# A loop over experts that takes two rounds at a time and gathers the tokens of both with one set of 256-column products

## The reference, cut to what matters

```python
def _moe(x, router, w_gate, w_up, w_down):
    xt = x.reshape(B * S, D)
    logits = (xt @ router).astype(jnp.float32)
    vals, ids = lax.top_k(logits, TOP_K)
    w = jax.nn.softmax(vals, axis=-1)
    gate = jnp.sum(jax.nn.one_hot(ids, N_EXPERTS, dtype=jnp.float32) * w[..., None], axis=1)
    out = jnp.zeros_like(xt)
    for e in range(N_EXPERTS):
        out = out + gate[:, e:e + 1].astype(xt.dtype) * _swiglu(xt, w_gate[e], w_up[e], w_down[e])
    return out.reshape(B, S, D)
```

## Time and profile before

| | |
|---|---|
| median of 3 runs | 2768.25 us (2766.36 to 2773.51) |
| the profiled execution | 2761.59 us, its span 2759.8 us |
| mean granted clock of TensorE | 0.988 of full speed |
| busy share of the span | TensorE 96%, VectorE 69%, ScalarE 55%, GpSimd 1% |
| moved from HBM | 578.8 MB, 210 GB/s over the span |
| expert rounds | 8, from 1751.83 to 2738.95 us of the span |

### The profile page before, as it was taken

One profiled execution on the slowest core, in us unless ns is written; L12 is line 12 of the kernel. 1 busy time (PEld: TensorE's weight loads), 2 busy tenths in 40 slices (PEclk: granted clock), 3 DMA queues, 4 the chain that ended last, 5 costly groups with the idle time before them and its releaser, 6 DMA issues.

```text
span 2759.8 us, 39481 instructions
## 1 busy us (share of the span) xinstructions
PE 2656.6 (96%) x14426; PEld 2179.9 (79%) x14426; DVE 1899.7 (69%) x2512; ACT 1515.8 (55%) x2207; POOL 18.1 (1%) x20
## 2 busy tenths in 40 slices
PE   7998999999998999989999999999999999999998
PEld 3754778888655999969999867888888888888887
DVE  2677555543258676575554656789898988989896
ACT  4223443222255544355444355678787877878785
POOL 0000000000000000000000100000000000000000
PEclk9999999999999999999999999999999999999999
DMA  6657122222220345314554222599899989889994
GB/s 259 238 198 310 62 92 92 103 96 92 92 77 31 138 170 183 137 62 153 184 184 153 107 77 107 210 347 379 338 373 354 365 349 370 350 338 375 346 370 168
DMA packets 80692, 581.53 MB, mean 211 GB/s; under 512 B 8896, under 2 KB 10176, under 8 KB 10176
## 3 DMA queue, kind: packets, MB, share of 16 engines
q1 hardware_dynamic: 80576, 579.90, 55.6%
HBM read 578.82 MB, written 1.05 MB: 210 GB/s over the span
## 4 chain that ended last, share of the span: by engine, by line
PE 87%; DVE 7%; ACT 3%; DMA 2%; issue 1%; POOL 0%; SPq 0%; ACTq 0%; DVEq 0%
PE ps L289 7%; PE ps L290 7%; PE ps L291 7%; PE ps L2483 7%; PE ps L2485 7%; PE ps L2484 7%; PE ps L2510 4%; PE ps L2512 4%; PE ps L2511 4%; PE ps L1118 3%; PE ps L1120 3%; PE ps L1119 3%; DMA ring<-in_stream_dram 2%; DVE parts L264 2%; PE ps L352 1%; PE ps L407 1%
## 5 line engine op out<-in xcount | busy, mean ns | idle before, releaser
L264 DVE TENSOR_TENSOR parts<-ring,parts 128x1024 fp32r<-128x1024 f32 x294 | 357.6, 1224 | 405.7 <-ACT parts L255 393.4
L255 ACT ACTIVATE parts<-ring 128x1024 fp32r<-128x1024 f32 x294 | 307.8, 1054 | 455.7 <-PE ps L291 195.7
L289 PE MATMUL ps<-parts 128*128 128x256 f32 (+1 forms) x1472 | 475.3, 323 | 7.9 <-DVE arena L1190 4.7
L290 PE MATMUL ps<-parts 128*128 128x256 f32 (+1 forms) x1472 | 470.7, 320 | 0.0
L291 PE MATMUL ps<-parts 128*128 128x256 f32 (+1 forms) x1472 | 470.3, 319 | 0.0
L2708 DVE TENSOR_TENSOR parts<-ring,parts 128x1024 fp32r<-128x1024 f32 x280 | 332.3, 1222 | 12.0 <-ACT parts L2551 0.4
L2551 ACT ACTIVATE parts<-ring 128x1024 fp32r<-128x1024 f32 x280 | 291.9, 1061 | 54.2 <-PE ps L2485 47.3
L289 PEld LDWEIGHTS ps<-parts 128*128 128x128 f32 x1472 | 281.3, 191 | 37.0 <-DVE arena L1190 8.1
L2483 PE MATMUL ps<-parts 128*128 128x512 f32 x752 | 296.8, 395 | 1.8 <-DVE parts L2708 1.8
L291 PEld LDWEIGHTS ps<-parts 128*128 128x128 f32 x1472 | 281.4, 191 | 19.8
L290 PEld LDWEIGHTS ps<-parts 128*128 128x128 f32 x1472 | 281.4, 191 | 19.6 <-issue 0.2
(11 more groups left out here) (400 smaller groups left out, 4692.3 us busy)
## 6 DMA issues: line engine op xcount, KB each, us to landing
ring<-in_stream_dram SPq DMA_DIRECT2D x380, 1024.0 KB, 5.8
h<-in_stream_dram SPq DMA_DIRECT2D x112, 1024.0 KB, 7.1
arena<-in_stream_dram SPq DMA_DIRECT2D x56, 1024.0 KB, 7.0
x<-in_x_dram SPq DMA_DIRECT2D x1, 2048.0 KB, 7.7
tab<-in_table_dram SPq DMA_DIRECT2D x1, 1724.5 KB, 11.7
out_dram<-x SPq DMA_DIRECT2D x4, 256.0 KB, 2.5
tab<-in_table_dram SPq DMA_DIRECT2D x1, 184.5 KB, 2.8
arena<-in_table_dram SPq DMA_DIRECT2D x1, 144.0 KB, 13.8
```

The costliest lines, as they stand in the source:

```text
L255: nc.scalar.activation(self.w_lead[:, self.buffer(g)], units(ring[:, n % NS, :])[:, g % UPS], ACT.Copy)\
L264: nc.vector.tensor_tensor(self.w_rest[:, self.buffer(g)], units(ring[:, n % NS, :])[:, g % UPS], self.w_lead[:, self.buffer(g)].bitcast(F3 ...
L289: nc.tensor.matmul(dst, wl[:, k, :], xl, start=(k == 0), stop=False)
L290: nc.tensor.matmul(dst, wl[:, k, :], xr, start=False, stop=False)
```

## The change

The loop now runs over pairs of rounds, and its body holds two rounds ("halves" 0 and 1) one behind the other. `Round(pair, half)` turns counts per round into semaphore values. The number of pairs is computed on VectorE beside the number of rounds, and an odd number of rounds is filled up with an empty one. `S_` has 256 columns, for the ranks of two rounds, and `select` makes all four blocks of it, in the second half alone. The gather is cut in two, `gather_lead` and `gather_rest`, 16 products of 256 columns each; both use banks 0 to 3, so `gather_rest` waits until ScalarE has copied the lead sums. In the second half the lead gather stands where the gather stood, at f = 14, and the rest gather stands at f = 18 (`LATE`); in the first half there is no gather. ScalarE and VectorE make four copies each (still 128 x 512) in the second half, VectorE's behind the cut of f = 23 (it was f = 19). There are two sets of `x_lead` and `x_rest`, the rests in a part of `x` that is free by then. Ahead of the loop, `gather_lead` comes before the six dummy products and `gather_rest` behind them. The places of `hidden_turn(NG - 1)`, `hidden_out(NG - 1)` and `hidden_rest(NG - 1)`, at f = 14, are the same in both halves.

```diff
@@ gather @@
-        def gather(eng):
-            for bank, tok in ((2, tok_lead), (0, tok_rest)):
-                for k in range(KD):
-                    for t in range(TT):
-                        mm = nc.tensor.matmul(ps[:, bank + k // 4, (k % 4) * P:(k % 4 + 1) * P], tok[:, t, k, :],
-                                              S_[:, t, :], start=(t == 0), stop=(t == TT - 1))
-                mm.then_inc(S("gathered"), 1)
+        def gather_lead(eng):
+            for k in range(KD):
+                for t in range(TT):
+                    mm = nc.tensor.matmul(ps[:, k // 2, (k % 2) * PS:(k % 2 + 1) * PS], tok_lead[:, t, k, :],
+                                          S_[:, t, :], start=(t == 0), stop=(t == TT - 1))
+            mm.then_inc(S("gathered"), 1)
+        def gather_rest(eng, pair):
+            for k in range(KD):
+                if k % 4 == 0:
+                    eng.wait_ge(S("x_lead"), pair * 4 + (2 * (k // 4) + 2))
+                for t in range(TT):
+                    mm = nc.tensor.matmul(ps[:, k // 2, (k % 2) * PS:(k % 2 + 1) * PS], tok_rest[:, t, k, :],
+                                          S_[:, t, :], start=(t == 0), stop=(t == TT - 1))
+            mm.then_inc(S("gathered"), 1)
@@ tensor, ahead of the loop @@
-            gather(eng)
+            gather_lead(eng)
...
+            gather_rest(eng, 0)
+            n = pair_count(eng)
@@ tensor, down cuts @@
                 for f in range(F2):
                     if f == F2 // 2:
                         hidden_turn(NG - 1)
-                        eng.wait_ge(S("sel"), r + 2)
-                        gather(eng)
+                        if at.half:
+                            eng.wait_ge(S("sel"), at.pair + 2)
+                            gather_lead(eng)
+                    if f == LATE and at.half:
+                        gather_rest(eng, at.pair + 1)
...
+            with eng.Fori(0, n) as pair:
+                for half in range(2):
+                    round_products(Round(pair, half))
@@ scalar @@
-                for m in range(2):
-                    tokens_lead(m, r + 1)
+                if at.half:
+                    tokens_lead(at.pair + 1)
@@ select, vector @@
+            for e in range(2):
+                for t in range(TT):
+                    ins = nc.vector.tensor_scalar(S_[:, t, e * P:(e + 1) * P], col("iota"), RK[:, t, of(e)], None,
+                                                  ALU.is_equal)
...
-                for i in range(NCU + F2 // 2, NCU + F2 // 2 + CUTS):
+                for i in range(NCU + F2 // 2, NCU + LATE + CUTS):
                     rest(i)
-                for m in range(2):
-                    tokens_rest(m, r + 1)
-                for i in range(NCU + F2 // 2 + CUTS, NC):
+                if at.half:
+                    tokens_rest(at.pair + 1)
+                for i in range(NCU + LATE + CUTS, NC):
                     rest(i)
```

More of the change, by code:

```diff
@@ L2325, in moe @@
         NCU, NC = 2 * NU, 2 * NSL
-        x_lead = parts[:, 0:UNIT].rearrange("p (k s) -> p k s", k=KD)
-        x_rest = parts[:, UNIT:2 * UNIT].rearrange("p (k s) -> p k s", k=KD)
+        x_leads, x_rests = ([parts[:, n * UNIT:(n + 1) * UNIT].rearrange("p (a b s) -> p a b s", a=4, b=2),
+                             x_r[:, 4 * n:4 * n + 4, T:NTOK].rearrange("p a (b s) -> p a b s", b=2)] for n in range(2))
         at = ARENA - 2 * F2 * P
@@ L2496, in tensor @@
                         mm.then_inc(S("sg_turn"), 1)
[L2498 removed]
+                eng.wait_ge(S("sum"), at(4, 6))
                 for f in range(F2):
@@ L2528, in scalar, with tokens_lead, outputs @@
             nc.scalar.activation(sm[:, 2:4], sm[:, 0:2], ACT.Exp).then_inc(S("exp"), 1)
[L2529 to L2537, removed]
+            def tokens_lead(pair):
+                eng.wait_ge(S("gathered"), pair * 2 + 1)
+                for n in range(2):
+                    for e in range(2):
+                        nc.scalar.activation(x_leads[e][:, 2 * n:2 * n + 2], gathered_half(n)[:, e], ACT.Copy)\
+                          .then_inc(S("x_lead"), 1)
+            def outputs(at):
+                eng.wait_ge(S("product"), at(NC, CUTS))
                 for n in range(2):
@@ L2699, in sums, with round_halves @@
                                             ALU.add).then_inc(signal, 1)
-            for m in range(2):
-                tokens_rest(m, 0)
-            n = round_count(eng)
-            with eng.Fori(0, n) as r:
+            tokens_rest(0)
+            n = pair_count(eng)
+            def round_halves(at):
                 def rest(i):
-                    eng.wait_ge(S("lead"), r * NC + (i + 1))
+                    eng.wait_ge(S("lead"), at(NC, i + 1))
                     nc.vector.tensor_tensor(w_rest[i % CUTS],
@@ L2744, in vector @@
                 hidden_rest(NG - 1)
-                for i in range(NCU + F2 // 2, NCU + F2 // 2 + CUTS):
+                for i in range(NCU + F2 // 2, NCU + LATE + CUTS):
                     rest(i)
-                for m in range(2):
-                    tokens_rest(m, r + 1)
-                for i in range(NCU + F2 // 2 + CUTS, NC):
+                if at.half:
+                    tokens_rest(at.pair + 1)
+                for i in range(NCU + LATE + CUTS, NC):
                     rest(i)
-            outputs(n)
-            sums(n, S("x"))
+            with eng.Fori(0, n) as pair:
+                for half in range(2):
+                    round_halves(Round(pair, half))
+            outputs(Round(n, 0))
+            sums(Round(n, 0), S("x"))
         return dict(name="moe", tensor=tensor, scalar=scalar, vector=vector, sync=extra_slots)
```

160 lines of the change are left out of this document (94 added, 66 removed).

## The result

The changed kernel takes 2799.51 us (median of 5 runs, 2792.79 to 2801.52). The kernel before, run beside it, takes 2771.31 us (5 runs, 2766.36 to 2780.71). The ratio is 1.0091, with a 95% interval of 1.0075 to 1.0108: slower by 0.9%, some 21 to 30 us. The forecast was 2781, with a range up to 2792. The direction was right and the size was not: the change costs about twice what the sum gave.

The account below looks back on a forecast made before the run. The prediction took the expert stage to be bound by TensorE's issue. Exposed cover +4.0, clock falls +6.4 and stage start +2.6 summed to +13.0 us on a median of 2768.25, giving 2781 us, range 2770 to 2792.

Parts of the forecast that it names:

- cover at f = 14 against the saved gather: At f = 14, exposed copy chain outweighs saved gather: first half 0.46 us shorter, second 1.45 longer; +4.0 us over four pairs.
- clock: TensorE's clock falls after three of four first-half stops and once at the stage's start, 1.6 us each: +6.4 us.
- start of the stage: Before the first round, two gathers and their copies delay TensorE's first product from 1751.83 to 1754.4: +2.6 us.
- back jumps: At the loop's end, the longer loop with half as many jumps back was taken to cost nothing.
- The gather alone, -13.6 us: In the loop, 32 products of 256 columns replace 7.22 us of gather per pair with 3.82: 13.6 us less over four pairs.
- ScalarE has stood idle 7.53 us when these transposes end: At f = 14, ScalarE waits for the last transposes; a 3.44 us chain to the cut follows, covered by the gather.
- What costs nothing: List of items put at no cost: selection, longer loop and its back jumps, DMA, register arithmetic for the waits.
- 3.5 us of queued products cover it: At the back jump, TensorE's sequencer jumps at 1872.3, the round's first product starts at 1875.81, so queued products hide it.
- The rival: Code loaded again at each of three back jumps, 0 to 3.6 us each; 2784 to 2796, likeliest 2788; chance 0.14.
- TensorE's issue: In the expert stage's rounds, what TensorE issues sets a round's cost; it is busy through all 123.3 us.

Follow-up runs that it names:

- all_short: The all_four kernel with 8 holding (unused) products at the stage's start instead of 14; 2761.57 us against 2771.52 before, ratio 0.9962.
- peeled: The order kernel with the first three pairs written out ahead of the loop, so no back jump is taken with 8 rounds; 2763.84 us.
- all_four: Changed kernel with the edits of order, place and peeled, plus 14 holding (unused) products behind the first rest gather; 2760.88 us against 2769.76 before, ratio 0.9966.
- order: Changed kernel with ScalarE and VectorE making the cuts of f = 14 to 19 ahead of the last hidden group's copies; 2773.31 us, ratio 1.0015 to before.
- order_before: The kernel before the change, with only the reordering of order (cuts of f = 14 to 19 ahead of the last hidden group's copies); 2767.02 us.
- unroll: Changed kernel's two-round loop kept, but each round gathers its own tokens as before, into the same place; 2788.47 us.
- place: The order kernel with the second half's tokens in the sixth slot buffer's columns of `arena_r`, and that buffer in free table columns; 2766.39 us.
- table: Changed kernel with the second half's tokens in free columns of the table `tab` instead of `x`; 2799.56 us.
- filled: Changed kernel with seven holding (unused) products behind the last transposes of each first half, in place of the stop; 2796.95 us.

## Why the prediction was right or wrong, point by point

The stage's 28.4 us, beside the 13.0 of the sum:

| term | forecast | measured | from |
|---|---|---|---|
| cover at f = 14 against the saved gather | +4.0 | +4.0 | pair of all_short (119.73, 123.59) and stops of 3.14 and 1.15, less 246.62, four times |
| clock | +6.4 | +9.5 | what is left of 28.4; its parts below |
| start of the stage | +2.6 | +2.4 | 26.90 - 24.46 |
| place of the second tokens | not in it | +7.2 | four second halves, 125.38 (peeled) - 123.59 (all_short) |
| back jumps | 0 | +5.3 | 1.87 + 1.96 + 2.19, less 3 x 0.23 |

- **The gather alone, -13.6 us: right.** Where nothing else is paid, the rounds take 985.6 us (all_four) against 999.2. A pair saves 3.3 us, forecast 3.4; the other 0.4 us are in round one, which is 0.3 us longer than the other first halves in all_four and 0.7 longer than the other rounds in the kernel before.
- **The cover: right, in size and place.** "ScalarE has stood idle 7.53 us when these transposes end": the chain behind them came out as forecast, four times 3.14 and four times 1.15 (1.24 forecast: the gather in front covers 1.99 us and not 1.91). order and order_before show it from two sides: where the gather covers the chain, its order is worth 0 us; where it doesn't, 24.7.
- **The clock: right in kind, low in size.** Three falls behind the long stops, as forecast, at 1.6 us each. The one at the start was twice as long (6.83 us, where the forecast took it for one like the others): round one takes 122.64 us in peeled, with this fall, and 120.01 in all_four, without it, so it costs 2.6. And one came behind a back jump, where the sum had no stop. (Round seven is as long as three and five: it had this fall, and none behind its own stop at f = 14.) 2.6 for the start and four times 1.6 are 9.0; the other 0.5 of the row stands in no single place.
- **The start: right.** Lead gather, copies and first cut came in the order of the working; 2.4 for 2.6.
- **"What costs nothing", back jumps: wrong.** The step that failed is "3.5 us of queued products cover it". The cover was nearly right (3.1 us, from 2016.5 to 2019.56), but the price of the jump was read from a jump within code that stays loaded, 0.21 us. 4.34 us of jump and 0.4 more to the first product leave 1.6 to 2.0 open. The rival had 0 to 3.6 us for each of three jumps and 2788 as its likeliest time: in kind and size it was what happened here (in unroll the same loop length cost 12.3). It was given 0.14, although the only row on it, five packets in round one and none later, told that the loop of before stays loaded and gave no reason why twice as much would. The windows count 1,166 products and weight loads in the body of before and 2,268 in the new one; the first moved packets in the first round alone (5), the second in every round (39 from 1900 to 2790). (The Trainium skill, page "Runtime: NRT & Kernel Launch", section "Instruction fetch mechanics", gives TensorE's instruction memory 128 KiB, 2048 instructions, and says that a taken branch whose target isn't in the current two-page window has to wait for a fetch. The traces agree with the first figure: 1,166 held, 2,268 not. A window of two of its 256-instruction pages does not fit the loop of 1,166, which moved no packet after the first round. The section has no price; here it was 4.34 us for TensorE's jump.)
- **The tokens' place: missing.** The diff puts the second half's tokens into `x_r`, and no sentence of the prediction costs that. "TensorE's issue" was taken as a number of products by one duration, 0.227 us, while that duration belonged to one place of the weights. It is the largest term that was missed, 7.2 us. None of the rows could have priced it with these shapes; it should have been named as an unknown, with its bounds.
- **The range.** 18.5 us lie between forecast and median: 7.2 + 5.3 + 3.1 (clock) - 0.2 (start) are 15.4, and 3.1 come from the kernel before, whose median over 5 runs was 3.1 us above that of the three runs the forecast started from. With every term but the place at its measured size the forecast would have been 2789.5, within the range; the place takes it over the end.

## What to carry to other kernels

Work that is to be saved on the bounding engine may be the cover of a chain on others; where the order of that chain is written by hand, mend the order first (here: the cuts ahead of the hidden group), since alone it cost nothing and with the saving it was worth 24.7 us. A loop made longer should be compared, engine by engine, with what stays loaded now; where the trip count is small, writing out the trips removed it. When a change moves an operand, look at the distance between the products that read it before and after: a busy engine hides such a loss from every view of waits.

## What the runs showed of the hardware that I had not expected

- 512-column products whose weight tile stands in `x` or `tab` start 0.2326 us apart; in `parts` or `arena_r` 0.2272. That is 2.4%, and nothing in the waits, the clock or the DMA share tells of it. Which property of the place does it is open.
- A back jump to code that isn't loaded takes TensorE's sequencer 4.34 us in the kernel after (at most 4.59), 5.1 to 5.2 in order, 5.6 to 6.4 in place and 5.8 to 6.4 in unroll, against 0.21 where the code is loaded. TensorE's stop, beyond an ordinary step, is that time less the products already queued (3.1 us in the kernel after, 3.5 in unroll, 4.0 in order and place), and 0.4 us more. What makes the jump longer or shorter is open. ScalarE stands 3.0 to 4.2 us at its own jump. Straight code of the same length has no such stop (peeled).
- The same stop doesn't always bring the clock down. Of the four stops of 3.14 us three did in the kernel after, and three in table, there not the first but the last. Of the stops at jumps, 2.19 (after), 2.27 (table), 2.31 (place), 2.90 and 3.47 us (unroll) did, and 2.18 (place), 2.73 (filled), 3.02 (place), 3.04 (unroll) and all from 1.74 to 2.06 did not. What decides between them no run here shows.
